# A fifteen-slot ring of expert weight chunks, its odd chunks loaded from ScalarE's DMA queue

## The reference

```python
def block_fn(args):                     # per block of 128 rows and expert e
    xb, e = args
    h = jax.nn.silu((xb @ w_gate[e]).astype(f32)) * (xb @ w_up[e]).astype(f32)
    return h.astype(dt) @ w_down[e]
...
out = jnp.zeros((T, x.shape[1]), f32).at[row_tok].add(ybuf.astype(f32) * row_w[:, None])
```

## Time and profile before

| | |
|---|---|
| median of three runs | 1884.53 us |
| the profiled execution | 1888.79 us, of it 1886.1 us span and 2.7 us around it |
| granted TensorE clock, mean | 0.976 of full speed |
| TensorE matmuls busy | 1785.5 us, 95% of the span |
| VectorE / ScalarE / GpSimd busy | 1056.1 / 779.1 / 490.0 us |
| experts, first gate matmul to last down matmul | 1262 to 1854 us |
| bytes moved over the span | 315.64 MB |

### The profile page before, as it was taken

The page is one execution under the profiler, slowest core; times in us unless marked ns, Lnnn a source line. Parts: engine busy times, 40 slices in busy tenths (PEclk is TensorE's granted clock), DMA queues, the critical chain, the costliest instruction groups (busy, mean ns, idle before and its releaser), DMA issues. The chain is left out here.

```text
span 1886.1 us, 25607 instructions
## 1 busy us (share of the span) xinstructions
PE 1785.5 (95%) x10085; PEld 1550.7 (82%) x10085; DVE 1056.1 (56%) x1224; ACT 779.1 (41%) x916; POOL 490.0 (26%) x282
## 2 busy tenths in 40 slices
PE   8999989999999999999999979959999999999992
PEld 6899989999999999999899968847777766667661
DVE  7565580002455444554611142448888888888884
ACT  4455460001122211122300032237787777777774
POOL 0332332223223222232222210012334332234210
PEclk9999999999999999999999989969999999999997
DMA  4111111223111111111122456438999999999995
GB/s 146 37 51 51 37 48 64 72 68 114 48 37 33 43 40 36 36 33 36 59 80 95 165 172 247 172 106 317 373 377 377 371 366 368 375 359 375 369 334 203
DMA packets 145552, 315.64 MB, mean 167 GB/s; under 512 B 10648, under 2 KB 105976, under 8 KB 120760
## 3 DMA queue, kind: packets, MB, share of 16 engines
q1 hardware_dynamic: 135608, 287.74, 42.0%
q0 software_dynamic: 9856, 26.66, 5.3%
HBM read 286.94 MB, written 35.29 MB: 171 GB/s over the span
## 5 line engine op out<-in xcount | busy, mean ns | idle before, releaser
L222 PE MATMUL job_ps<-xn_hi,w_hi 128*128 128x352 f32 x1536 | 512.1, 333 | 4.1 <-DVE xn_lo L400 3.8
L224 PE MATMUL job_ps<-xn_hi,w_lo 128*128 128x352 f32 x1536 | 495.5, 323 | 0.0
L223 PE MATMUL job_ps<-xn_lo,w_hi 128*128 128x352 f32 x1536 | 494.6, 322 | 0.0
L222 PEld LDWEIGHTS job_ps<-xn_hi,w_hi 128*128 128x128 f32 x1536 | 290.1, 189 | 8.8 <-issue 5.6
L223 PEld LDWEIGHTS job_ps<-xn_lo,w_hi 128*128 128x128 f32 x1536 | 290.8, 189 | 2.6 <-issue 0.3
L224 PEld LDWEIGHTS job_ps<-xn_hi,w_lo 128*128 128x128 f32 x1536 | 290.0, 189 | 0.0
L206 POOL CAST w_hi<-w_raw 128x1024 fp32r<-128x1024 f32 x78 | 83.5, 1070 | 783.1 <-issue 464.8
L2112 DVE TENSOR_TENSOR ex_w_lo<-u,ex_w_hi 128x2048 fp32r<-128x2048 f32 x96 | 217.8, 2286 | 27.1 <-ACT ex_w_hi L2022 26.8
L2112 DVE TENSOR_TENSOR ex_w_lo<-h_raw_more,ex_w_hi 128x2048 fp32r<-128x2048 f32 x96 | 217.9, 2286 | 19.8 <-ACT ex_w_hi L2022 19.5
L2022 ACT ACTIVATE ex_w_hi<-u 128x2048 fp32r<-128x2048 f32 x96 | 183.8, 1917 | 71.2 <-DMA u<-in_w_chunks 30.5
L2022 ACT ACTIVATE ex_w_hi<-h_raw_more 128x2048 fp32r<-128x2048 f32 x96 | 184.6, 1924 | 65.3 <-DMA h_raw_more<-in_w_chunks 27.7
(11 more groups left out here) (288 smaller groups left out, 3069.6 us busy)
## 6 DMA issues: line engine op xcount, KB each, us to landing
u<-in_w_chunks SPq DMA_DIRECT2D x96, 1024.0 KB, 17.1
h_raw_more<-in_w_chunks SPq DMA_DIRECT2D x96, 1024.0 KB, 17.9
w_raw<-in_w_in SPq DMA_DIRECT2D x64, 512.0 KB, 4.0
u<-in_x_columns SPq DMA_DIRECT2D x6, 704.0 KB, 7.1
merged_lru<-gate SPq DMA_DIRECT2D x8, 528.0 KB, 4.7
spare<-merged_lru SPq DMA_DIRECT2D x8, 528.0 KB, 5.5
merged<-gate SPq DMA_DIRECT2D x8, 528.0 KB, 4.7
w_raw<-in_w_lru_o SPq DMA_DIRECT2D x8, 512.0 KB, 3.8
```

The source lines that it names most:

```text
L222: pe.matmul(out, M.w_hi[s][:, k, :], x_hi[:, k, cols], start=(k == 0), stop=False)
L223: pe.matmul(out, M.w_hi[s][:, k, :], x_lo[:, k, cols], start=False, stop=False)
L224: mm = pe.matmul(out, M.w_lo[s][:, k, :], x_hi[:, k, cols], start=False, stop=(k == KD - 1))
```

## The change

The ring of chunks becomes 15 slots deep. Room for it comes from writing the low part over the chunk itself: every slot is addressed twice, as float32 (what the DMA fills) and as the rounded format (`view_twice`), and `w_lo` no longer has buffers of its own. A slot is therefore free only when TensorE has used the chunk, and the loads wait on `used` in place of `lo_done`. Slots 8 to 14 are new buffers of the expert stage (`ex_raw`); their first loads are issued at its start without a wait, and the wait for `xe_in[0]` is gone. From chunk 16 on, SP issues the even chunks (and the last three), and ScalarE issues the odd ones on its own DMA queue, each behind one of its casts: after the cast of chunk n it issues chunk n+12. The load of the last norm's gain moves behind the chunk loads. Some scratch tiles of late parts share buffers now.

```diff
 class Chunks:
-    RAW = 8
+    FIRST = 8
+    RAW = 15
     SPLIT = 3
...
-def load_chunk(sp, A, H, e, c, n):
+def load_chunk(eng, A, H, e, c, n):
     b = n % Chunks.RAW
-    sp.dma_start(H.raw[b], A["w_chunks"][e, c]).then_inc(H.raw_in[b], 16)
+    eng.dma_start(H.raw[b][0], A["w_chunks"][e, c]).then_inc(H.raw_in[b], 16)
...
-        w_lo = [sb(f"w_lo{c}", [P, CHUNK_W], F32R) for c in range(SPLIT)]
+        H.raw += [view_twice(nc, ctx, f"ex_raw{c}", CHUNK_W) for c in range(Chunks.FIRST, RAW)]
+        raw, w_lo = [x for x, _ in H.raw], [x for _, x in H.raw]
...
             def _(sp):
-                sp.dma_start(g_fin[:], A["norm_final_g"].partition_broadcast(P)).then_inc(g_in, 16)
-                sp.wait_ge(xe_in[0], 16)
+                for n in range(Chunks.FIRST, RAW):
+                    load_chunk(sp, A, H, *Chunks.ORDER[n], n)
                 for n in range(RAW, N_CHUNKS):
-                    sp.wait_ge(lo_done, n - RAW + 1)
-                    load_chunk(sp, A, H, *Chunks.ORDER[n], n)
+                    if n % 2 == 0 or n >= N_CHUNKS - SPLIT:
+                        sp.wait_ge(used, n - RAW + 1)
+                        load_chunk(sp, A, H, *Chunks.ORDER[n], n)
...
+                sp.wait_ge(router.over_set, 1)
+                sp.dma_start(g_fin[:], A["norm_final_g"].partition_broadcast(P)).then_inc(g_in, 16)
...
-                        lo = w_lo[n % SPLIT][:].rearrange("p (k n) -> p k n", k=4)
+                        lo = w_lo[n % RAW].rearrange("p (k n) -> p k n", k=4)
...
-                    act.activation(w_hi[n % SPLIT][:], H.raw[n % RAW], ACT.Copy).then_inc(hi_done, 1)
+                    act.activation(w_hi[n % SPLIT][:], raw[n % RAW], ACT.Copy).then_inc(hi_done, 1)
+                    follow = n - SPLIT + RAW
+                    if n >= SPLIT and follow % 2 and follow < N_CHUNKS - SPLIT:
+                        load_chunk(act, A, H, *Chunks.ORDER[follow], follow)
...
-                    dve.tensor_tensor(w_lo[n % SPLIT][:], H.raw[n % RAW], w_hi[n % SPLIT][:].bitcast(F32),
+                    dve.tensor_tensor(w_lo[n % RAW], raw[n % RAW], w_hi[n % SPLIT][:].bitcast(F32),
                                       ALU.subtract).then_inc(lo_done, 1)
...
+def view_twice(nc, ctx, name, width):
+
+    with ExitStack() as plain:
+        x = plain.enter_context(nc.sbuf_tensor(name, [P, width], F32))
+    return x[:], ctx.enter_context(nc.sbuf_tensor(f"{name}_lo", [P, width], F32R))[:]
```

More of the change, by code:

```diff
@@ L170, in __init__ @@
         self.xn_lo = sb("xn_lo", [P, KD, T], F32R)
-        self.u = R.u[:].rearrange("p (k t) -> p k t", k=KD)
+        self.u = R.u.rearrange("p (k t) -> p k t", k=KD)
         self.w_raw = [sb(f"w_raw{s}", [P, KD, P]) for s in range(2)]
@@ L259, in normalise @@
         sem = lambda n: R.spend(keep.enter_context(nc.semaphore(f"nm_{n}")))
-        x = R.u[:].rearrange("p (c k t) -> p c k t", c=CT, k=KD)
+        x = R.u.rearrange("p (c k t) -> p c k t", c=CT, k=KD)
         sq = [sb(f"square{b}", [P, KD, CW]) for b in range(2)]
@@ L1263, in __init__, with late @@
         st = Steps(None, step)
-        def late(ctx, slot_bank):
+        def late(ctx, slot_bank, scratch):
             self.pm = slot_bank[0:SLOTS, 0:E]
+            self.over_x = scratch
             sl = lambda n, sh: ctx.enter_context(nc.sbuf_tensor(f"rt_{n}", sh, F32))
             self.hw = [sl(f"hot_w{k}", [P, NTILE, E]) for k in range(2)]
-            self.over_x = sl("over_x", [1, E, E])
         def choose(dve, ts):
@@ L1376, in weigh_over @@
             st.link(dve.tensor_scalar(ones[:], R.const[0:1, CN_IOTA:CN_IOTA + E], 1.0, None, ALU.add))
-            st.link(dve.tensor_tensor(self.over_x[:], over_n[:].unsqueeze(1).broadcast_to((1, E, E)),
+            st.link(dve.tensor_tensor(self.over_x, over_n[:].unsqueeze(1).broadcast_to((1, E, E)),
                                       ones[:].unsqueeze(2).broadcast_to((1, E, E)), ALU.is_equal))
-            st.link(dve.tensor_tensor(self.over_x[:], self.over_x[:],
+            st.link(dve.tensor_tensor(self.over_x, self.over_x,
                                       R.const[0:1, CN_IOTA:CN_IOTA + E].unsqueeze(1).broadcast_to((1, E, E)),
                                       ALU.mult))
-            st.link(dve.tensor_reduce(over_f[:, 0:E], self.over_x[:], AX.X, ALU.add))
+            st.link(dve.tensor_reduce(over_f[:, 0:E], self.over_x, AX.X, ALU.add))
             dve.tensor_copy(H.over[:], over_f[:]).then_inc(self.over_set, 1)
@@ L1522, in _ @@
                         sp.wait_ge(w_lo_done, KD)
-                    if t - 2 < Chunks.RAW:
+                    if t - 2 < Chunks.FIRST:
                         load_chunk(sp, A, H, *Chunks.ORDER[t - 2], t - 2)
-                for c in range(NTILE - 2, Chunks.RAW):
+                for c in range(NTILE - 2, Chunks.FIRST):
                     load_chunk(sp, A, H, *Chunks.ORDER[c], c)
@@ L1736, in experts @@
         LAST = E - 1
-        router.late(ctx, py[1])
+        g_fin = sb("fi_g", [P, D])
+        router.late(ctx, py[1], g_fin[0:1, :].rearrange("p (a b) -> p a b", a=E))
         osem = lambda n: ctx.enter_context(nc.semaphore(f"ov_{n}"))
@@ L1743, in experts @@
         ov_xt, ov_y = xe[0], y[0]
-        ov_x_t, ov_hid_t = sb("ov_rows_t", [P, KD, P]), sb("ov_hidden_t", [P, KF, P])
+        ov_x_t = xe[1][:].rearrange("p (k n) -> p k n", k=KD)
+        ov_hid_t = y[1][:, 0:KF * P].rearrange("p (k n) -> p k n", k=KF)
         ov_w_now = sb("ov_w_now", [P, 1])
@@ L1755, in experts @@
         warm = sb("fi_warm", [1, 1])
-        junk, g_fin = sb("fi_square", [P, D]), sb("fi_g", [P, D])
+        junk = y[1]
         ss, rms, rstd = (sb(f"fi_{n}", [P, NTILE]) for n in ("sum_sq", "rms", "rstd"))
@@ L1819, in _ @@
                 start_at_one(sp, (ov_x_in, 16))
-                sp.wait_ge(lo_done, N_CHUNKS)
+                sp.wait_ge(used, N_CHUNKS)
                 over_experts(sp, each)
@@ L1933, in down @@
                         hi = w_hi[n % SPLIT][:].rearrange("p (k n) -> p k n", k=2)
-                        lo = w_lo[n % SPLIT][:].rearrange("p (k n) -> p k n", k=2)
+                        lo = w_lo[n % RAW].rearrange("p (k n) -> p k n", k=2)
                         for k in range(2):
@@ L2202, in __init__ @@
         self.eps = sb("eps", [P, 1])
-        self.u = sb("u", [P, KD * T])
+        self.u, self.u_lo = view_twice(nc, ctx, "u", KD * T)
         self.w_out_in = ctx.enter_context(nc.semaphore("w_out_in"))
@@ L2218, in __init__ @@
         sb = lambda n, s, d=F32: ctx.enter_context(nc.sbuf_tensor(f"h_{n}", s, d))
-        self.more = sb("raw_more", [P, 4 * CHUNK_W])
-        self.raw = [x[:, c * CHUNK_W:(c + 1) * CHUNK_W] for x in (R.u, self.more) for c in range(4)]
+        self.more, more_lo = view_twice(nc, ctx, "raw_more", 4 * CHUNK_W)
+        self.raw = [tuple(x[:, c * CHUNK_W:(c + 1) * CHUNK_W] for x in pair)
+                    for pair in ((R.u, R.u_lo), (self.more, more_lo)) for c in range(4)]
         self.raw_in = [ctx.enter_context(nc.semaphore(f"raw_in{c}")) for c in range(Chunks.RAW)]
```

## The result

The changed kernel takes 1914.62 us (median of four runs, 1913.33 to 1917.66 us), the kernel before 1884.28 us in the same comparison. The ratio is 1.0165, 95% interval 1.0146 to 1.0184. The forecast had the sign and the loop that sets the step; +30 us stand against +10, outside the range that I gave. The profiled execution has a span of 1912.3 us, 26.2 us more than before.

What follows compares the result with a forecast made beforehand. Full DMA engines bound the late expert stage once the chunk cushion was gone. Row-loop steps of 18.7 us gave +11.5 us, less 1.5 us of chunk stall: +10 us, 1894 us by the median; range 1867 to 1912 us.

Steps and rivals of the forecast that it cites:

- the loop that sets the step: GpSimd's expert-stage loop through memory: store, index copy, gather, turning on TensorE; about 1 us of slack in two steps.
- What bounds before: Expert stage: TensorE's pace, 17.68 us a step, while the chunk cushion lasts; then full DMA engines, 18.71 us on average.
- What there was to win: Expert stage: 17.5 us of stalls to expert 31; if nothing else changed, 16 us faster in all.
- The start: Seven chunk loads issued at the expert stage's start delay the first gather and so the whole stage by 2.5 us.
- my bound of 19 us: Expert stage: the early start of chunk loads adds up to 19 us of cushion, part of it lost again.
- Depth: Chunk ring: loads issued 15 ahead of TensorE instead of 11 at best, about 12 us of cushion.
- ScalarE's issues: Chunk issues on ScalarE take 0.33 us and hide in idle time before casts; unlikely bound 1.8 us a step.
- What the second queue adds: A second loaded chunk queue delays store by 2.1 and gather by 2.4 us, half of what one queue adds.
- rival C: Second queue costs as much as the first, 9 us on the row loop: 21.7 us a step, 1972 us; 0.10 including halfway.
- The step that failed: Row loop needs 19.4 us, but chunk queues sometimes run empty, so steps settle at 18.7 us from about step 5.
- my own formula: Row loop's step: two steps of 35.36 us, less 1.0 us slack, plus added store and gather latency, divided by two.
- the halfway one under rival C: Row loop keeps 19.4 us a step all the way, 18 us more, 1912 us; shares chance 0.10 with rival C.

## Why the prediction was right in kind and wrong in size

**What bounds before: right.** Opening the loop there is worth nothing; more depth on one queue takes most of the chunk waits away.

**What there was to win: nearly right.** I gave 16 us for the full gain; one queue with the open loop wins 12.3 us by the medians of its comparison, and its stage is 14.1 us shorter. My 17.5 us of stalls counted the step with VectorE's router code as one that a deeper ring could win, 5.7 us in the kernel before. My 18.71 us for full DMA engines is an average over that step, over five steps of 17.7 us behind it, and over others. It came out right all the same: the last three steps, which wait for chunks, take 18.7 to 18.9 us.

**The start: right in its term.** The first rows are turned 1259.6 - 1251.6 = 8.0 us behind the issue of their gather, in place of 5.7: +2.3 us against my 2.5. The turning began at 1259.6 us nevertheless and not at 1262, since GpSimd issued the gather 2.2 us earlier than in the profile of before, in a part that the change doesn't touch. That the early start adds cushion was right too: it takes 12.1 us off ScalarE's waits for chunks, of which the stage feels 2.8 us. How much of my bound of 19 us it holds, no run tells.

**Depth: near.** About 12 us of cushion was my figure for four chunks; ring 15 against ring 11 gives 1885.2 - 1876.5 = 8.7 us, and 9.2 us of stage.

**ScalarE's issues: right for this kernel.** They take 0.334 us there, start beside the cast (at 1441.93 us, with the cast at 1441.92) and hide. With all chunks on ScalarE, or with half loads, some take far longer there (up to 5.37 and 6.75 us), which I had not thought of.

**What the second queue adds: 4.5 us expected, 3.7 measured** (12.7 - 9.8 and 11.4 - 10.6 us), but by luck. I took half of the first queue's price because the backlog in all would be the same, and the runs show that this isn't what counts: on one queue the stores land in 9.8 us whether chunks take 19.9, 25.6 or 32.9 us. And 12.7 us is a median over stores of 5.6 to 15.4 us. With the loop open the second queue adds 3.9 us to a gather alone (12.9 against 9.0 us), nearer to rival C.

**The step that failed** is the sentence that the extra latency shrinks when the chunk queues run empty at times, so that the step settles where the engines are just full, 18.7 us. Nothing settles. From 1437 to 1509.5 us TensorE never waits and turns rows every 17.6 to 17.8 us, while the stores, issued one a step, land in 8.7, 11.1, 12.7, 13.1 and 14.9 us (the first and the last):

```profile
DMA to landing us min/median/max: 8.7/8.7/8.7
...
DMA to landing us min/median/max: 14.9/14.9/14.9
```

Then the rows come too late, TensorE waits 3.2 us, and this step takes 21.1 us; the store behind it lands in 9.4 us and it begins again. Busy time in this stretch, and behind the wait that ends at 1577.5 us (columns as in the earlier trace rows):

```profile
1437.00:1509.50 72.50, 72.50 (x346) 51.49 (x345) 63.46 (x44) 57.78 (x49) 21.99 (x12) 1.00 1.01 373
1577.50:1590.90 13.40, 13.32 (x51) 9.52 (x52) 6.16 (x5) 6.82 (x7) 1.20 (x3) 0.76 0.70 245
```

Between waits the DMA engines are full (1.01) and the latency grows; only behind a wait, when TensorE has freed no slot for some time, do they run short (0.70) and the latency shrinks. So the relief that I counted on has to be paid for first with a wait, and the mean step is 19.21 us. Of the ten waits seven are of 2.6 to 4.1 us and three under 0.9 us, where I expected 1 us in most steps. Why the stores get slower from step to step, while the chunks land in 9 to 13 us from the second of these stores on, was not tried by itself. The gather comes later and lies more and more beside the store, which is one candidate; the store that goes out right behind a late gather is the slowest (15.4 us).

The loop kept its price, then. With the measured 3.7 us my own formula gives (35.36 - 1.0 + 3.7) / 2 = 19.0 us a step, and 26 steps of 19.0 in place of 18.7 are 8 us more. I had worked out a case like this, as the halfway one under rival C (19.4 us a step, 1912 us), gave it and C together 0.10, and set the range to end at it.

**The rest of the size** is mostly the clock, which the formula left out. From expert 2 to 31 it takes 557.1 us against 29 x 17.68 = 512.7 without stalls, 44.4 us more. TensorE's waits in 1292 to 1850 us are 25.2 us for rows and 3.3 us once for a low part (VectorE's router code), 28.5 us. The clock of 0.97 over 558 us is 0.03 x 558 = 16.7 us. Together 45.2 us, all of it within the rounding of 0.97. The granted clock falls to 0.50 behind each of the eight waits of 2.6 us or more, for 3.4 us, or 6.8 us behind the longest (1577.0 to 1583.8 us), and stays at 1.00 behind the three under 0.9 us. There TensorE's part of the loop runs slower too, which lengthens the loop it waits for: the turning takes 1.54 in place of 0.66 us, a matmul of the down projection 0.43 in place of 0.23.

## What to carry to other kernels

Before you give bulk loads a second queue, look for small transfers on a third that lie in a loop, and compute that loop with the latency each more loaded queue adds: here 2.9 us on a store and 0.8 us on a gather, by medians, made a gain of 0.4% a loss of 1.65%. If a loop through memory has 1 us of slack, open it before you add load to its queues (eight index buffers in place of four were worth 36 us with two queues, and nothing in the kernel before), and put depth into one queue. When a loop's price and a bandwidth limit lie close together, don't let the loop settle at the limit by argument: it can run at full speed for some steps and then pay in one lump, and the lump costs clock as well (here 0.50 for 3.4 to 6.8 us behind each wait of 2.6 us or more). And before you count stalls as winnable, look at what ends the longest of them.

## What the runs showed of the hardware

A row transfer's delay goes with the packets of the chunk queues and not with their backlog: 9.8 us (one queue, 8 KB packets, chunks landing in 32.9 us), 12.7 us (two queues, 8 KB, 10.8 us), 9.9 us (two queues, 4 KB, 31.0 us), 8.3 us (one queue, 4 KB). The limit of this is the cycle above, in which stores of one kernel with two queues range from 8.7 to 15.4 us.

The single packets in the trace fit. It doesn't name a packet's engine, but the differences between start times of 4 KB row packets (0.33 us for half of them, 0.15 to 0.25 us for most others) pile up at 0.62 us beside one queue of 8 KB packets (0.31 us each), at 0.93 us beside two (the kernel with the open loop), at 0.47 us beside one of 4 KB (0.16 us each) and at 0.63 us beside two of those. That is one packet of each loaded queue between two row packets. In the changed kernel, where chunks land in 10.8 us and not in 34.2 as with the open loop, they pile up at 0.31, 0.62 and 0.93 us: beside none, one or both of the queues, as this would have it when they run empty at times.

I had not expected that an issue can block. With eleven slots on one queue every chunk issue takes 0.33 us, with fifteen on one queue some take up to 6.1 us:

```profile
L1705 SPq DMA_DIRECT2D ex_raw<-in_w_chunks x45: 327/328/328, 1325.4 to 1798.7; - x45
```

(one queue on SP, ring 11), and with ring 15

```profile
L1705 SPq DMA_DIRECT2D ex_raw<-in_w_chunks x78: 327/328/6107, 1301.1 to 1796.1; - x78
```
